# The convolution mixer's input projection as seven block products per chunk instead of eight (Strassen–Winograd form), with the weight sums shared by GpSimd and VectorE

## What is computed

```
h = rmsnorm(x, norm_mix[0])               # 288 tokens x 1024
z = h @ conv_w_in                         # (1024, 4096)
b_gate, c_gate, v = z[:, 0:1024], z[:, 1024:2048], z[:, 2048:3072]
q_x = z[:, 3072:]                         # queries of the cross-attention
y = causal_conv(c_gate * v, state, w)     # three taps; the last rows of c_gate*v go out
mix = b_gate * y
xa  = cross_attn(q_x, mem_k, mem_v)
x   = x + concat(mix, xa) @ w_out
```

## Time and profile before

| | before |
|---|---|
| time, median of 3 | 1193.41 us |
| span of the profiled execution | 1192.3 us |
| projection of the mixer (L932 of layer 0) | 66.76 to 191.2 us, 512 records |
| TensorE matmul busy in the span | 95% |
| VectorE, ScalarE, GpSimd busy | 30%, 13%, 1% |

### The profile page before, as it was taken

How to read it: one execution, slowest core, us unless ns; L and a number is a source line. 1 busy time by engine, 2 the same in 40 slices (tenths; PEclk the granted TensorE clock), 3 DMA queues, 4 the chain that set the end, 5 groups by cost and what they waited for, 6 DMA issues and landing times.

```text
span 1192.3 us, 14370 instructions
## 1 busy us (share of the span) xinstructions
PE 1136.3 (95%) x6182; PEld 708.4 (59%) x6182; DVE 362.0 (30%) x894; ACT 154.9 (13%) x366; POOL 11.8 (1%) x22
## 2 busy tenths in 40 slices
PE   8999999999999999979999999999999999997885
PEld 6567777776765454435656656466677764543333
DVE  5222223211214141344234242523401023432225
ACT  2000002101211010120201011011200021110002
POOL 0000000000000000000000000000000000000000
PEclk9999999999999999999999999999999999999888
DMA  9963336933999999999336656392998459999994
GB/s 370 427 235 128 124 124 278 413 142 113 419 411 428 425 425 428 425 426 387 148 144 254 245 187 266 142 362 106 413 422 352 167 208 381 428 427 428 428 427 168
DMA packets 30323, 364.63 MB, mean 306 GB/s; under 512 B 3520, under 2 KB 3664, under 8 KB 7472
## 3 DMA queue, kind: packets, MB, share of 16 engines
q1 hardware_dynamic: 27360, 339.86, 69.8%
q10 hardware_dynamic: 1712, 19.17, 3.9%
q0 software_dynamic: 1184, 4.63, 1.0%
HBM read 339.32 MB, written 24.32 MB: 305 GB/s over the span
## 4 chain that ended last, share of the span: by engine, by line
PE 84%; DMA 13%; DVE 1%; issue 1%; ACT 1%; SPq 0%; DVEq 0%
PE bank L932 24%; PE bank L595 13%; DMA ring<-in_gu 11%; PE bank L737 7%; PE bank L1016 5%; PE bank L484 5%; PE bank L478 4%; PE bank L780 4%; PE bank L748 3%; PE bank L709 3%; DMA ring<-in_vc 2%; PE bank L987 1%; PE bank L1097 1%; PE bank L498 1%; PE bank L1078 1%; PE bank L469 1%
## 5 line engine op out<-in xcount | busy, mean ns | idle before, releaser
L932 PE MATMUL bank<-hT,ring 128*128 128x288 f32 x1088 | 268.2, 407 | 1.0 <-issue 1.0
L932 PEld LDWEIGHTS bank<-hT,ring 128*128 128x128 f32 x1088 | 205.7, 190 | 66.9 <-issue 12.0
L595 PE MATMUL bank<-arena,ring 128*128 128x288 f32 x592 | 146.4, 406 | 0.0
L737 PE MATMUL bank<-ring,arena 128*32 128x512 f32 x888 | 108.5, 624 | 25.9 <-DMA ring<-in_gu 25.7
L595 PEld LDWEIGHTS bank<-arena,ring 128*128 128x128 f32 x592 | 111.2, 190 | 29.6 <-issue 0.2
L737 PEld LDWEIGHTS bank<-ring,arena 128*32 128x32 f32 x888 | 28.4, 112 | 96.7 <-issue 75.7
L780 PE MATMUL bank<-arena 128*128 128x288 f32 x256 | 68.9, 413 | 3.2 <-issue 2.8
L1585 DVE TENSOR_TENSOR xT<-xT,bank 128x288 f32<-128x288 f32 x128 | 58.2, 455 | 38.1 <-PE bank L780 34.4
L780 PEld LDWEIGHTS bank<-arena 128*128 128x128 f32 x256 | 46.2, 190 | 24.4 <-issue 8.3
L709 PE MATMUL bank<-arena 128*128 128x256 f32 x256 | 60.6, 390 | 0.0
L1016 PE MATMUL bank<-ring,hT 128*128 128x512 f32 x128 | 57.2, 597 | 0.0
(11 more groups left out here) (269 smaller groups left out, 929.0 us busy)
## 6 DMA issues: line engine op xcount, KB each, us to landing
ring<-in_gu SPq DMA_DIRECT2D x55, 2048.0 KB, 19.6
ring<-in_dn SPq DMA_DIRECT2D x28, 2048.0 KB, 20.0
ring<-in_rin SPq DMA_DIRECT2D x14, 2048.0 KB, 13.7
ring<-in_cin SPq DMA_DIRECT2D x8, 2048.0 KB, 27.4
ring<-in_kc SPq DMA_DIRECT2D x8, 2048.0 KB, 8.1
ring<-in_vc SPq DMA_DIRECT2D x8, 2048.0 KB, 10.3
ring<-in_st SPq DMA_DIRECT2D x8, 2048.0 KB, 10.5
out_rs<-ring ACTq DMA_DIRECT2D x8, 2048.0 KB, 8.3
```

Of the source, the lines that this page charges most:

```text
L595: mm = pe.matmul(bank[1 + o % 4][:, 0:T], w[k], cat[:, k, :], start=(k == 0), stop=(k == kt - 1))
L737: mm = pe.matmul(bank[2][32 * e:32 * e + 32, :], xt[:, k, 32 * e:32 * e + 32], w[2 * e + kk], start=(k == 0), stop=(k == KD - 1), skip_gro ...
L932: mm = pe.matmul(outs[o], w[:, o, k, :], src[:, k, :], start=(k == 0), stop=(k == KD - 1))
```

## The change

The 8 × 4 grid of one chunk's product is cut in halves three times: weights into outputs {c_gate, v} and {b_gate, q_x}, and into input features k = 0..3 and 4..7; tokens into 0..143 and 144..287. That makes a 2 × 2 by 2 × 2 block product, done with seven half-size products in place of eight. Each has 2 outputs × 4 k = 8 matmuls of 144 token columns.

- The host lays `cin` out in four quarters of 1024 words, one per weight block. The host adds nothing.
- Per chunk, four sums of weight quarters: GpSimd makes `sums[0]` (`first_sum`) and `sums[2]`, VectorE makes the third quarter in place (`s3`) and `sums[1]` (`s2`) in `next_sums`.
- Once, before the chunks, four sums of halves of the input (`mixed[0..3]`, 576 elements each) on VectorE.
- Per chunk, the outputs are put together from the banks: ScalarE copies bank `top` to `kept` (first product), `top` to `u_sb` (fourth), `fifth` to `kept`, and q_x from `z` to `qx`; VectorE makes the five sums of `outputs` (named `c11`, `u3`, `c22`, `c21`, `c12`). The taps then read from SBUF, after `c12`, which waits for the seventh product.
- The zeroing of `qm_` (2304 elements) goes from VectorE, ahead of the chunks, to GpSimd, behind them. TensorE's wait for the value copies (`v_out`) goes from chunk 0 to chunk 1. A ring slot is released after the sixth product and `sums[2]`. Several semaphores are merged (`outputs_stored`, `mixer_stored`, `chosen`, the `cat_out` wait as a chained wait), with waits for the same events.

```diff
+            def product(out, w, x, first):
+                for o in range(2):
+                    for k in range(4):
+                        mm = pe.matmul(out[:, o, :], w[:, o, k, :], x[:, k, :], start=(first and o == 0 and k == 0),
+                                       stop=(k == 3), skip_group_check=True)
+                mm.then_inc(S("cin_sum"), 1)
+
+            def conv_in(c):
+                top, side, third, fifth = cin_banks(c)
+                landed(pe, ("cin", c))
+                if c == 1:
+                    pe.wait_ge(S("v_out"), 4)
+                if c >= 2:
+                    pe.wait_ge(S("mixing"), mixed_by("c12", c - 2))
+                product(top, cin_quarter(c, 0), hT[:, 0:4, 0:half_t], True)
+                product(side, cin_quarter(c, 1), hT[:, 4:8, 0:half_t], True)
+                pe.wait_ge(S("mixing"), mixed_by("s3", c))
+                product(third, cin_quarter(c, 2), mixed[2], True)
+                pe.wait_ge(S("mixing"), mixed_by("s2", c))
+                pe.wait_ge(S("kept"), 3 * c + 1)
+                product(top, sums[1], mixed[1], False)
+                pe.wait_ge(S("sums"), 2 * c + 1)
+                if c >= 2:
+                    pe.wait_ge(S("kept"), 3 * (c - 2) + 3)
+                product(fifth, sums[0], mixed[0], True)
+                pe.wait_ge(S("mixing"), mixed_by("c11", c))
+                product(side, cin_quarter(c, 3), mixed[3], True)
+                pe.wait_ge(S("sums"), 2 * c + 2)
+                pe.wait_ge(S("kept"), 3 * c + 2)
+                product(top, sums[2], hT[:, 4:8, half_t:T], False)
 # ScalarE, per chunk
-                act.activation(c_sb[c % 2], bank[4 * (c % 2)][:, 0:T], ACT.Copy).then_inc(S("c_out"), 1)
-                act.activation(qx[:, c, :], bank[4 * (c % 2) + 3][:, 0:T], ACT.Copy).then_inc(S("qx_out0"), 1)
+                act.wait_ge(S("mixing"), mixed_by("c12", c - 1))      # for c > 0
+                act.activation(kept, top, ACT.Copy).then_inc(S("kept"), 1)
+                act.activation(u_sb, top, ACT.Copy).then_inc(S("kept"), 1)
+                act.activation(kept, fifth, ACT.Copy).then_inc(S("kept"), 1)
+                act.activation(qx[:, c, :], z[:, 3, :], ACT.Copy).then_inc(S("qx_out0"), 1)
 # VectorE
+            def next_sums(c):
+                landed(dve, ("cin", c))
+                dve.wait_ge(S("sums"), 2 * c + 1)
+                dve.tensor_tensor(cin_quarter(c, 2), cin_quarter(c, 0), cin_quarter(c, 2), ALU.subtract) \
+                   .then_inc(S("mixing"), 1)
+                dve.tensor_tensor(sums[1], sums[0], cin_quarter(c, 0), ALU.subtract).then_inc(S("mixing"), 1)
+            def outputs(c):
+                dve.tensor_tensor(z[:, 0:2, 0:half_t], kept, side, ALU.add).then_inc(S("mixing"), 1)
+                dve.tensor_tensor(u_sb, u_sb, third, ALU.add).then_inc(S("mixing"), 1)
+                dve.tensor_tensor(z[:, 2:4, half_t:T], u_sb, kept, ALU.add).then_inc(S("mixing"), 1)
+                dve.tensor_tensor(z[:, 2:4, 0:half_t], u_sb, side, ALU.add).then_inc(S("mixing"), 1)
+                if c + 1 < 8:
+                    next_sums(c + 1)
+                dve.tensor_tensor(z[:, 0:2, half_t:T], kept, top, ALU.add).then_inc(S("mixing"), 1)
...
-            V_(dve.memset(qm_, 0.0))
 # GpSimd
+            first_sum(0)
             store_memory()
+            pool.wait_ge(S("kv_sum"), 8)
+            for c in range(8):
+                if c:
+                    pool.wait_ge(S("cin_sum"), 7 * c)
+                pool.wait_ge(S("mixing"), mixed_by("s2", c))
+                pool.tensor_tensor(sums[2], cin_quarter(c, 1), sums[1], ALU.subtract).then_inc(S("sums"), 1)
+                pool.wait_ge(S("cin_sum"), 7 * c + 5)
+                if c + 1 < 8:
+                    first_sum(c + 1)
+            pool.memset(qm_, 0.0).then_inc(S("queries_zeroed"), 1)
```

More of the change, by code:

```diff
@@ L157, in v3, with v4 @@
             return ap.rearrange("p (k t) -> p k t", k=k)
+        def v4(ap, o, k):
+            return ap.rearrange("p (o k n) -> p o k n", o=o, k=k)
         HM1, KTO, VO, SQO, CATO, PHO, QMO = 0, 2048, 4096, 6144, 8448, 15360, 18688
@@ L173, in build @@
         qm_diag = qm.rearrange("p h (b x) -> p h b x", x=TD + NS)[:, :, :, 0:NS]
-        c_sb = [ar(SQO + 288 * i, T) for i in range(2)]
+        half_t = T // 2
+        quarter = SLOT // 4
+        sums = [v4(ar(o, quarter), 2, 4) for o in (QMO, QMO + quarter, CATO + 8 * T)]
+        mixed = [v3(ar(CATO + 16 * T + 2 * T * i, 2 * T), 4) for i in range(4)]
+        z = v3(ar(CATO + 8 * T + quarter, 4 * T), 4)
+        kept = v3(ar(PHO + 2752, T), 2)
+        u_sb = v3(ar(PHO + 2752 + T, T), 2)
         full = [ar(SQO + 576 + 306 * i, 306) for i in range(2)]
@@ L326, in wait_used, with mixed_by, cin_quarter, cin_banks @@
             eng.wait_ge(S(sem), v)
+            if k == "cin":
+                eng.wait_ge(S("sums"), 2 * c + 2)
+        MIXING = {"c11": 1, "u3": 2, "c22": 3, "c21": 4, "s3": 5, "s2": 6, "c12": 7}
+        def mixed_by(what, c):
+            if what in ("s3", "s2"):
+                return ("s3", "s2").index(what) + 1 if c == 0 else 2 + 7 * (c - 1) + MIXING[what]
+            return 2 + 7 * c + ({"c12": 5}[what] if c == 7 and what == "c12" else MIXING[what])
+        def cin_quarter(c, q):
+            return v4(slot(AT[("cin", c)] % R)[:, q * quarter:(q + 1) * quarter], 2, 4)
+        def cin_banks(c):
+            return [v3(bank[4 * (c % 2) + n][:, 0:T], 2) for n in range(4)]
         @block.sync
@@ L952, in _ @@
             pe.wait_ge(S("kt_out"), 2)
-            pe.wait_ge(S("v_out"), 4)
             pe.wait_ge(S("normed"), NORM_DONE["mix0"])
[L956 to L961, removed]
+            def product(out, w, x, first):
[27 more added lines that the diff above has]
+                product(top, sums[2], hT[:, 4:8, half_t:T], False)
             for c in range(8):
-                project_in("cin", c, hT, conv_drained)
-            pe.wait_ge(S("conv_out"), 7)
+                conv_in(c)
+            pe.wait_ge(S("mixing"), mixed_by("c12", 6))
             pe.wait_ge(S("qx_out0"), 7)
@@ L1918, in _ @@
             experts(1)
[L1919 to L1921 removed]
+            pool.wait_ge(S("outputs_stored"), 32 + 48)
+            pool.wait_ge(S("mixer_stored"), 32)
+            pool.wait_ge(S("mixer_stored"), 32 + 16 * H)
             pool.wait_ge(S("keys_stored0"), 16)
             pool.wait_ge(S("values_stored0"), 16)
[L1924 removed]
             for b in range(2):
```

98 lines of the change are left out of this document (61 added, 37 removed).

## The result

The changed kernel takes 1184.25 us (median of 5 runs, 1181.59 to 1187.18), the kernel before 1194.26 us in the same session (5 runs, 1192.39 to 1198.92). The ratio is 0.9916, with a 95% interval of 0.9897 to 0.9935: faster by 0.65 to 1.0%. In a second session it took 1184.99 us (6 runs) against 1194.18 (11 runs), ratio 0.9906 [0.9884, 0.9929]. The forecast was 1180.3, 13.1 us less; the measured gain is about 10 us in the first session and 9 in the second. The profiled execution of the changed kernel is the fastest of all 11: 1181.59 us, with a span of 1179.8 where 1179.2 was forecast. How near these two spans lie says little, since the median execution took some 3 us more.

A forecast was written before the change was run, and what follows sets the result against it. TensorE was taken to bound the kernel, its mixer projection unbroken for 124.40 us; −14.4 − 1.1 + 2.4 = −13.1 us on a span of 1192.3 gave 1179.2, so 1180.3 us; range 1177.5 to 1188, own range 1178 to 1183.

The forecast's parts named there:

- Term 1: Mixer projection on TensorE: seven half-size products, 896 records at 122.5 ns, take 109.8 us instead of 124.2; −14.4 us.
- Term 2: Start of the projection: only chunk 1 still waits for VectorE's last value copy; −1.1 us.
- Term 3: VectorE inside a chunk: 7.9 us of work in 13.73, every result ready in time; 0 us.
- Term 4: GpSimd's weight sums: no cost to TensorE while one sum stays below 5.5 us; 0 us.
- Term 5: End of the projection: TensorE idles while the query copy waits behind the last sums and taps; +2.4 us.
- Rival A: Projection: 0.17 us lost at each of 40 product starts on waits, 6.8 us back, 1187 us; chance 0.05.
- C: As a rival: weight loads bind at short columns in the projection; 1187 us at 130 ns, 1202 at 147; chance 0.05.
- Rival B: GpSimd's sums bound the chunks, costing 7 × (2G + 2.6 − 13.73), G us per sum; 1200 us at G = 7; chance 0.07.
- the lock's formula: GpSimd and two-input VectorE operations exclude each other: about 8 × (G − 3.2) us lost, gain gone at G = 4.8.
- Rival D: Later stages, DMA bound parts starting no earlier, return the gain; all returned would be 1193 us; chance 0.03.
- The distance from span to time: Whole kernel: the median time was taken as 1.1 us above the profiled span, 1179.2 giving 1180.3 us.
- every later stage 13 us earlier: Sign expected after the projection: all following stages shift earlier by 13 us with TensorE.

The follow-up runs named there:

- values_first: The changed kernel with TensorE's wait for the value copies put back ahead of chunk 0: 1183.94 us.
- all_vector: The changed kernel with all four weight sums of a chunk on VectorE, none on GpSimd: 1186.22 us, ratio 0.9926 to the kernel before.
- quarter_columns: The changed kernel with each matmul of the seven products made as two of 72 columns: 1276.49 us.
- before_halved: The kernel before, eight block products kept, each projection matmul cut into two of 144 columns: 1194.43 us beside 1194.54.
- pool_twice: The changed kernel with every GpSimd weight sum made twice, one after the other: 1211.92 us, before 1194.54.

## Why the prediction was right, and what was off

The terms are those of the prediction's sum.

- **Term 1**, the seven products (−14.4): 109.78 us for 109.8 forecast, and 14.6 us less than before. The step that mattered was to take the rate from how far starts lie apart, not from durations: 406 ns and 190 ns records would have given a loss.
- **Term 2**, the start (−1.1): it came 1.0 us earlier against the value products, and undoing it costs 1.1 us (values_first).
- **Term 3**, VectorE in a chunk (0): no TensorE wait in the projection. VectorE is busy 80 us there where the forecast had 8 × 7.9 = 63; 26 us of the 80 are the lock (all_vector). The smallest slack was given as 3.2 us; `c11` came 2.3 us ahead of its product. The term held, with less room than worked out.
- **Term 4**, GpSimd (0): G is 2.36 us. The forecast took its value near VectorE's 1.22; the estimate from the Trainium skill, "GPSIMD Engine Reference" (3.1 Elementwise), 2.3 us, was the better one. Either lies under the bound.
- **Term 5**, the end (+2.4): the decode scores start 3.97 us behind the last product (178.78 − 174.81), forecast 4.05, before 1.66. That is +2.3.
- **Rival A** (gaps at gated products) is refuted by the unbroken piece of 896 records, **C** (loads bind) by its 122.3 ns; by quarter_columns' floor C would begin at (111.6 − 2.5) / 0.8335, an estimated 131 columns. **Rival B** (GpSimd becomes the bound) is not what happened, but its prices were wrong: with doubled sums the gain was lost and 17 us more, where the lock's formula still left some of it. The step that failed in it is that an operation was assumed to be held once per sum in its way, not every small operation once.
- **Rival D** (later stages return the gain) was given 0.03 and no share of the sum. Part of it is what happened. In two profiles stage B returned 1.3 and 6.5 us of 13.3. From the output projection to the end (B and C) the two profiles with the old code take 969.5 and 969.9 us, and all eleven with the change take longer, 971.4 to 977.8. Of that, 1.0 to 1.6 us is the idle piece, present each time. The rest is open. D's own mechanism, stages bound by the DMA that start no earlier, is not seen: the first load of expert weights inside B is issued at 283.8 and 283.9 us instead of 297.8. Waits for `in_gu` over the whole span are 25.7 and 27.0 us with the old code and 25.3 to 30.7 with the change, so they are part of it in some profiles only. Busy time at a lower granted clock differs without the change as well (in B 313.3 us before, 315.4 in before_halved), and in the second session the mean granted clock was 0.988 over 11 executions before and 0.987 over 6 after, by an estimate worth 1 us.
- **The distance from span to time** was taken as 1.1 us, from a median of other executions. It is 1.8 us: 1181.59 for a span of 1179.8, and the same in before_halved (1194.43 and 1192.6). The sum of 1179.2 would have been 1181.0 us.

So the term that was mis-sized is the one left out, "every later stage 13 us earlier": between 1181.0 and the median of 1184.25 lie 3.3 us. What stands between the profile (span 1179.8) and the median can only be the parts outside A, if A repeats as it does in the profiles.

For the total this leaves some luck. The prediction gave its own forecast 1178 to 1183 us, and both medians, 1184.25 and 1184.99, lie above that. They lie in the wider range because it had been opened for A, mild C and mild B, of which none happened. In stage A, where the mechanism is, 13.3 us for 13.1 is not luck: each part was measured by itself.

## What to carry to other kernels

When TensorE bounds a stage without a gap, a Strassen–Winograd form gave nearly its eighth here (14.6 us of 124.4; an eighth is 15.6, and half-length work costs 1.3 us for eight products). Two things had to hold: the halved matmuls stay above the rate of weight loads, and the last output sums don't lie in front of what TensorE needs next (here they did, for 2.3 us). Read both before writing it, and put what the next stage needs first (here one copy of 0.29 us, worth 2.3 us). Give GpSimd an elementwise sum only where VectorE has few operations beside it: count VectorE's small operations that keep all their data in SBUF, not its microseconds. And leave room in the forecast for the stages behind: here they returned 3 to 4 us in the median, most of it unexplained.

## What the runs showed of the hardware that was not expected

- A VectorE operation that has all its data in SBUF, beside a GpSimd sum, lasts until the sum ends, however small it is: 0.42 us became 2.38, and a copy of 16 elements with a single input took 2.32. One that reads a bank kept its 0.44 us. The Trainium skill, "SBUF — State Buffer" (SBUF: two separate sides), has this for VectorE operations with two SBUF inputs and for its two-port modes. That the two engines then nearly alternate, one held operation for each sum, is what pool_twice adds.
- A lock can make the helped engine busier: VectorE 80 us with GpSimd's help, 72 without.
- Full weights of 128 × 128 can follow each other every 111.6 ns under running matmuls, at records that show 192 ns.
- Behind 6.0 us of idle time TensorE's granted clock was 0.50 in the next 4 us.
- An idle piece of 1.0 to 1.6 us, put to no engine and no DMA, stands behind exactly 11 records of a stage whose matmuls did not change; its cause is open.
